# Two transformer layers on one core: the second branch turns moved behind pair 3's query turns, and the last expert's result handled in quarter pieces

## The reference

```python
for l in range(DEPTH):
    h = rms_norm(x, mix_norm_g[l])
    z = h @ w_in[l]                 # u, v (gMLP), c_q, c_kv, k_r (attention), gates
    y_a = gmlp_branch(u, v, ...) @ gm_w_proj[l]      # "pa": u * (W_s v + b), 8 groups
    y_b = mla_branch(c_q, c_kv, k_r, ...) @ mla_w_proj[l]   # "pb": 16 heads, causal
    gates = sigmoid(z[..., OFF_GATE:])
    x = x + (gates[0] * y_a + gates[1] * y_b) @ w_out[l]
    h2 = rms_norm(x, ffn_norm_g[l])
    if l % 2 == 0:
        x = x + swiglu(h2, dense_w_gu, dense_w_down)
    else:                           # top 2 of 8 by router, softmax weights
        for e in range(8):
            y = y + combine[:, e:e+1] * swiglu(h2, w_gu[e], w_down[e])
        x = x + y
```

## Time and profile before

| | us |
|---|---|
| median of 3 runs | 1450.35 (1450.29 to 1450.68) |
| profiled execution | 1450.41 |
| its span | 1448.7 |
| PE busy | 1438.9 |
| DVE busy | 1160.6 |
| ACT busy | 964.0 |

### The profile page before, as it was taken

One profiled execution on the slowest core, in us unless ns is written; L12 is line 12 of the kernel. 1 busy time (PEld: TensorE's weight loads), 2 busy tenths in 40 slices (PEclk: granted clock), 3 DMA queues, 4 the chain that ended last, 5 costly groups with the idle time before them and its releaser, 6 DMA issues.

```text
span 1448.7 us, 19542 instructions
## 1 busy us (share of the span) xinstructions
PE 1438.9 (99%) x6850; PEld 1187.5 (82%) x6850; DVE 1160.6 (80%) x1144; ACT 964.0 (67%) x1053; POOL 44.5 (3%) x53
## 2 busy tenths in 40 slices
PE   9999999999999999999999999999999999999998
PEld 7888788888888888878888888888888888888886
DVE  6977756665546977656998999999989899899997
ACT  6676754444435676754677777777777777777775
POOL 2000003000000000000200000000000000000300
PEclk9999999999999999999999999999999999999999
DMA  9473348955465463447799999999999999999995
GB/s 341 150 237 117 116 149 302 332 178 177 156 219 177 149 230 116 144 147 272 301 394 380 390 361 395 395 361 395 364 394 395 352 401 373 388 391 359 372 368 218
DMA packets 212316, 414.95 MB, mean 286 GB/s; under 512 B 14188, under 2 KB 55528, under 8 KB 212248
## 3 DMA queue, kind: packets, MB, share of 16 engines
q1 hardware_dynamic: 206232, 393.42, 75.0%
q0 software_dynamic: 4976, 16.97, 3.5%
q10 hardware_dynamic: 1040, 3.68, 0.6%
HBM read 398.20 MB, written 15.81 MB: 286 GB/s over the span
## 4 chain that ended last, share of the span: by engine, by line
PE 98%; ACT 1%; DVE 1%; DMA 0%; issue 0%; SPq 0%; ACTq 0%
PE ps L534 89%; PE ps L1083 1%; PE ps L957 1%; PE ps L935 1%; PE ps L795 1%; PE ps L944 1%; PE ps L915 1%; PE ps L934 0%; PE ps L884 0%; PE ps L1064 0%; DMA xres<-in_x 0%; ACT act_hi L1243 0%; PE ps L928 0%; PE ps L850 0%; PE ps L1075 0%; PE ps L913 0%
## 5 line engine op out<-in xcount | busy, mean ns | idle before, releaser
L504 DVE TENSOR_TENSOR w_lo<-raw,w_hi 128x2048 fp32r<-128x2048 f32 (+1 forms) x242 | 515.8, 2141 | 151.4 <-ACT w_hi L499 147.3
L499 ACT ACTIVATE w_hi<-raw 128x2048 fp32r<-128x2048 f32 (+2 forms) x241 | 433.6, 1801 | 215.2 <-PE ps L534 198.1
L534 PE MATMUL ps<-w_hi,act_hi 128*128 128x512 f32 (+1 forms) x1264 | 332.7, 393 | 1.3 <-ACT act_hi L1243 1.1
L534 PE MATMUL ps<-w_hi,act_lo 128*128 128x512 f32 (+1 forms) x1264 | 328.0, 388 | 0.0
L534 PE MATMUL ps<-w_lo,act_hi 128*128 128x512 f32 (+1 forms) x1264 | 325.0, 387 | 0.0
L534 PEld LDWEIGHTS ps<-w_lo,act_hi 128*128 128x128 f32 x1264 | 235.5, 188 | 48.8 <-DVE w_lo L504 0.5
L534 PEld LDWEIGHTS ps<-w_hi,act_lo 128*128 128x128 f32 x1264 | 235.0, 188 | 48.2
L534 PEld LDWEIGHTS ps<-w_hi,act_hi 128*128 128x128 f32 x1264 | 231.0, 188 | 47.0 <-ACT act_hi L1243 1.6
L499 ACT ACTIVATE w_hi<-raw_more 128x2048 fp32r<-128x2048 f32 x96 | 170.7, 1778 | 65.5 <-PE ps L534 64.0
L504 DVE TENSOR_TENSOR w_lo<-raw_more,w_hi 128x2048 fp32r<-128x2048 f32 x96 | 201.1, 2110 | 14.3 <-ACT w_hi L499 12.9
L504 DVE TENSOR_TENSOR w_lo<-raw_low,w_hi 128x2048 fp32r<-128x2048 f32 (+1 forms) x64 | 128.9, 2022 | 12.4 <-ACT w_hi L499 11.3
(11 more groups left out here) (286 smaller groups left out, 1278.7 us busy)
## 6 DMA issues: line engine op xcount, KB each, us to landing
raw<-in_moe_w_gu SPq DMA_DIRECT2D x192, 512.0 KB, 9.7
raw_more<-in_moe_w_gu SPq DMA_DIRECT2D x96, 512.0 KB, 10.0
raw<-in_w_in SPq DMA_DIRECT2D x72, 512.0 KB, 4.5
raw_low<-in_moe_w_gu SPq DMA_DIRECT2D x64, 512.0 KB, 9.6
raw_more<-in_moe_w_down SPq DMA_DIRECT2D x64, 512.0 KB, 6.2
raw<-in_dense_w_gu SPq DMA_DIRECT2D x44, 512.0 KB, 4.9
raw_low<-in_moe_w_down SPq DMA_DIRECT2D x32, 512.0 KB, 8.1
raw<-in_moe_w_down SPq DMA_DIRECT2D x32, 512.0 KB, 5.8
```

The source lines that it names most:

```text
L499: nc.scalar.activation(w_hi[:, self.split_slot(j), 0:n], self.raw(j)[:, 0:n], ACT.Copy).then_inc(self.hi, 1)
L504: nc.vector.tensor_tensor(w_lo[:, c, 0:n], self.raw(j)[:, 0:n], w_hi[:, c, 0:n].bitcast(F32), ALU.subtract).then_inc(self.lo, 1)
L534: return nc.tensor.matmul(dst, a, b, start=start and n == 0, stop=stop and n == 2)
```

## The change

In the mixer's list, for both layers, `a_turns` 1 leaves the second `gb` chunk and goes into the first `pa` chunk, behind its first three matmuls; `qk_turns` 3 and pair 2's normalisation stand in the `gb` chunk at 5 instead of 6.

```diff
         mul(l, "gb", 1, 4, [("split_lo", l, len(chunks) - 2), *slot(4, exps=False), ("k_scale", l, 1), split("split_lo"),
                             ("softmax", l, 3), evac("gb", 1)], split=False,
-            inside=[(2, ("exps", l, 2)), (5, ("a_turns", l, 1)), (6, turn(3)), (6, ("norm_probs", l, 2)),
+            inside=[(2, ("exps", l, 2)), (5, turn(3)), (5, ("norm_probs", l, 2)),
                     (6, split("split_hi"))])
         mul(l, "pa", 0, 0, [*slot(5, exps=False), split("split_lo"), ("softmax", l, 4)],
-            inside=[(4, turn(4)), (4, split("split_hi"))])
+            inside=[(1, ("a_turns", l, 1)), (4, turn(4)), (4, split("split_hi"))])
```

In the last expert, the last pass of (piece 1, half 0) goes behind the last pass of (piece 0, half 1), and the second half of the result is copied by ACT, scattered by PE, and for the second tile of positions added by DVE and stored by SP, in quarters of 256 columns:

```diff
-        END_ORDER = ((0, 0, (0, 1, 2)), (0, 1, (0, 1)), (1, 0, (0, 1, 2)), (0, 1, (2,)), (1, 1, (0, 1, 2)))
+        END_ORDER = ((0, 0, (0, 1, 2)), (0, 1, (0, 1)), (1, 0, (0, 1)), (0, 1, (2,)), (1, 0, (2,)), (1, 1, (0, 1, 2)))
+        LAST = ((0, 0, 512), (1, 0, 512), (0, 512, 1024), (1, 512, 768), (1, 768, 1024))
...
+            def store_last():
+                for i, (t, c0, c1) in enumerate(LAST):
+                    sp.wait_ge(pass_sems[0]["over"], i + 1)
+                    sp.dma_start(out[0, t * P:(t + 1) * P, c0:c1], xres[:, t, c0:c1]).then_inc(out_stored, 16)
...
-                        if (d, hf) == (1, 0):
+                        if (d, hf, passes[-1]) == (1, 0, 2):
                             mm.then_inc(z["half_done"], 1)
...
-                    pe.wait_ge(z["y_half1"], 1)
                     for t in range(TT):
-                        nc.tensor.matmul(ps[:, 2 + t, :], put[:, t * P:(t + 1) * P], y_sb[:, 512:1024], start=True, stop=True
-                                         ).then_inc(z["scattered"], 1)
+                        for quarter, ready in enumerate((z["y_half1"], z["y_end"])):
+                            if not t:
+                                pe.wait_ge(ready, 1)
+                            c = 256 * quarter
+                            bank = (2, 2, 3, 4)[2 * t + quarter]
+                            nc.tensor.matmul(ps[:, bank, c:c + 256], put[:, t * P:(t + 1) * P],
+                                             y_sb[:, 512 + c:768 + c], start=True, stop=True).then_inc(z["scattered"], 1)
...
-                        copy(y_sb[:, 512:1024], ps[:, 7, :], slot_w[:, 0:1]).then_inc(z["y_half1"], 1)
+                        copy(y_sb[:, 512:768], ps[:, 7, 0:256], slot_w[:, 0:1]).then_inc(z["y_half1"], 1)
+                        copy(y_sb[:, 768:1024], ps[:, 7, 256:512], slot_w[:, 0:1]).then_inc(z["y_end"], 1)
...
+                def last_scattered():
+                    for i, (t, c0, c1) in enumerate(LAST):
+                        dve.wait_ge(z["scattered"], (1, 2, 4, 5, 6)[i])
+                        if not c0:
+                            dve.wait_ge(rows_added[1][t], 16)
+                        bank, b0 = ((0, 0), (1, 0), (2, 0), (3, 0), (4, 256))[i]
+                        tt(xres[:, t, c0:c1], xres[:, t, c0:c1], ps[:, bank, b0:b0 + c1 - c0], ALU.add).then_inc(z["over"], 1)
```

More of the change, by code:

```diff
@@ L452, in decoder_trunk @@
                 "eturn_free1", "y_copied", "y_stored", "xs_landed", "first_turned", "first_hi", "first_lo", "slot_read",
-                "put_ready", "put_turned", "put_copied", "half_done", "y_half0", "y_lo", "y_half1", "scattered", "over")})
+                "put_ready", "put_turned", "put_copied", "half_done", "y_half0", "y_lo", "y_half1", "y_end", "scattered", "over")})
         class Ring:
@@ L687, in expert_loads @@
                     r.load(sp, e, GU_CHUNKS + d, [(to[:, 0:half], a), (to[:, half:2 * half], b)])
+            def store_last():
+                for i, (t, c0, c1) in enumerate(LAST):
+                    sp.wait_ge(pass_sems[0]["over"], i + 1)
+                    sp.dma_start(out[0, t * P:(t + 1) * P, c0:c1], xres[:, t, c0:c1]).then_inc(out_stored, 16)
             def store_out(z):
                 for i, (t, hf) in enumerate(TAIL):
-                    sp.wait_ge(z["over"], i + 1 if z is pass_sems[0] else len(TAIL) * (E - 1) + i + 1)
+                    sp.wait_ge(z["over"], len(TAIL) * (E - 1) + i + 1)
                     sp.dma_start(out[0, t * P:(t + 1) * P, hf * 512:(hf + 1) * 512],
@@ L700, in _ @@
             expert_loads(moe_ring, 0, E - 1, True)
-            store_out(pass_sems[0])
+            store_last()
             with sp.If(crowded > P):
-                sp.wait_ge(out_stored, 16 * len(TAIL))
+                sp.wait_ge(out_stored, 16 * len(LAST))
                 sp.dma_start(xs[:], x_rows[0, 1]).then_inc(pass_sems[1]["xs_landed"], 16)
@@ L710, in _ @@
                 store_out(pass_sems[1])
-                sp.wait_ge(out_stored, 2 * 16 * len(TAIL))
-            sp.wait_ge(out_stored, 16 * len(TAIL))
+                sp.wait_ge(out_stored, 16 * (len(LAST) + len(TAIL)))
+            sp.wait_ge(out_stored, 16 * len(LAST))
         @block.gpsimd
@@ L1230, in _ @@
             with pe.If(crowded > P):
-                pe.wait_ge(pass_sems[0]["over"], len(TAIL))
+                pe.wait_ge(pass_sems[0]["over"], len(LAST))
                 moe_pass(moe_ring2, 1)
@@ L2013, in scattered @@
                         dve.wait_ge(z["scattered"], len(TAIL) * (n - 1) + i + 1)
-                        if not q and not hf:
-                            dve.wait_ge(rows_added[1][t], 16)
                         xh = xres[:, t, hf * 512:(hf + 1) * 512]
@@ L2053, in body @@
                             ALU.subtract).then_inc(z["y_lo"], 1)
-                        scattered(1)
+                        last_scattered()
                     elif q:
@@ L2074, in _ @@
             with dve.If(crowded > P):
-                dve.wait_ge(out_stored, 16 * len(TAIL))
+                dve.wait_ge(out_stored, 16 * len(LAST))
                 link(ts(place, place, -float(P), None, ALU.add))
```

## The result

| | before | after |
|---|---|---|
| median, 6 runs each, same chip | 1450.64 (1450.29 to 1452.91) | 1457.05 (1456.74 to 1458.96) |
| profiled execution / its span | 1450.41 / 1448.7 | 1457.01 / 1455.2 |
| ratio | | 1.0045 [1.0035, 1.0055] |

The change costs 6.4 us. The forecast was +4.8 (1455.1, range 1453.0 to 1456.6): the direction is right, the size is outside the range. Of the 1.95 between 1455.1 and 1457.05, 0.3 is that the kernel before has a median of 1450.64 here and had 1450.35 over the three runs that the forecast started from.

A forecast was written before the change was run, and what follows sets the result against it. The prediction took TensorE (PE) to bound the kernel, busy 99% of the span. It added +4.98 us for both layers' waits and -0.2 for the tail to 1450.35, giving 1455.1, range 1453.0 to 1456.6.

The forecast's parts named there:

- What bounds: Whole kernel: PE bounds it, busy 99% of the span and 98% of the chain of work that ended last.
- A: Start of the first matmul of the first `pa` chunk, 584.56 in layer 1 before; forecast to come 1.57 us earlier.
- `t_lo` at A + 5.97: On DVE, the moved `t_lo` starts 5.97 us after A, behind nine instructions that run without a hole.
- +2.49 for a layer: First `pa` chunk: PE waits for `t_lo` at pair 4's query turns, which makes each layer 2.49 us longer.
- the 0.70 saved: Before A, waits around the old place of the branch turns go away, saving 0.70 us a layer.
- The clock: PE's granted clock stays at 1.00 around the turns; a fall to 1.2 GHz got chance 0.04, 5 us a layer.
- The tail, -0.2: Last matmuls, adds and stores: the last add and last store come some 0.2 us sooner, taken as -0.2.
- The upper bound of +0.9: Tail: nothing saved, and the extra issue and smaller packets cost as much as 0.9 us.
- The sum: Whole kernel: +4.98 for both layers and -0.2 for the tail give +4.8 us, 1455.1.
- (a): Pair 4's turns: banks are free before PE asks, only savings count, -1.6 us, 1448.8; chance 0.06.
- (b): Pair 4's turns: the wait is shorter or one layer's is partly absorbed, +2.5 us, 1452.9; chance 0.08.
- (c): Behind the new wait PE's clock falls to 1.2 GHz, 5 us a layer, 1465; chance 0.04.

The follow-up runs named there:

- Part 4: turns_only with pair 4's query turns nine matmuls sooner (turn_sooner, 1463.97 us) or nine later (turn_later, 1453.12 us).
- part 5: turns_only with the weight split and pair 3's exponentials and normalisation moved behind the branch turns; 1448.85 us, ratio 0.9989.
- turns_only: The kernel before with only the moved turns, the tail as before; 1456.39 us, ratio 1.0045.
- turns_again: turns_only, unchanged, run a second time; 1457.7 us, ratio 1.0043 against before.
- lo_first: The kernel of part 5: turns_only with the weight split and pair 3's exponentials and normalisation behind the branch turns; 1448.85 us, ratio 0.9989.
- turn_sooner: turns_only with pair 4's query turns nine matmuls sooner, right behind the branch turns; 1463.97 us, ratio 1.0086 against before.
- turn_later: turns_only with pair 4's query turns nine matmuls later; 1453.12 us, ratio 1.0011 against before.
- fill_eight: turns_only with 8 unused identity turns on PE ahead of pair 4's turns; 1455.78 us, ratio 1.0039 against before.
- fill_wait: turns_only with 20 unused identity turns on PE ahead of pair 4's turns; 1455.15 us, ratio 1.0035 against before.
- tail_only: The kernel before with only the tail's new matmul order and quarter pieces, the turns as before; 1450.76 us, ratio 1.0004.
- order_only: The kernel before with only the new order of the last matmuls; copies, adds and stores as before; 1450.46 us, ratio 1.0.

## Why the prediction was wrong

**What bounds, and A: right.** A was to come 1.57 earlier; corrected for the shift ahead of it, it came 1.51 + 0.13 = 1.64 earlier in layer 0, and 584.56 + 3.97 - 586.88 = 1.65 in layer 1.

**`t_lo` at A + 5.97: right**, 5.95 and 5.94. It was read from nine DVE instructions without a hole, and holds in both layers. Part 4 shows that `t_lo` stays there wherever PE asks for it, part 5 that it comes sooner, and the wait is gone, when the steps ahead of it on DVE and ahead of `t_hi` on ACT are moved.

**+2.49 for a layer: right at full clock**, 2.40 in layer 1 and 2.38 to 2.41 in the layers of `turns_only` and of the two filled waits. It is the wait of 2.83, plus 0.28 between the halves, less the 0.70 saved: 2.41.

**The clock: this step failed.** I wrote that the granted clock is 1.00 and that PE has no wait of 3 us here, and gave the fall 0.04, all or nothing, at 5 us a layer. But a row of 1.00 in a stretch with no wait says nothing of what follows a wait of 2.8. It fell in one layer of the profiled execution of after, in both of `turns_again`, in none of `turns_only`, so in three of six passages seen. The mean clock is 0.998 or less in five of the six executions of after, and in none of the 69 of before that were run beside the experiments. Nor was the price right: I took the 24 matmuls of a whole chunk, but only the eight turns and 12 matmuls stand behind the wait, and the clock comes back among the 12. So it took 1.45 to 1.47 (3.4 us at the low level) or 2.68 (6.9 us), not 5.

For the profiled execution the clock is 1.47 of what lies over the forecast. For the median it is only likely: the waits and the tail give 1450.64 + 4.81 + 0.23 = 1455.7, and two layers with an even chance of some 1.5 each are about the 1.4 that is left. But the one execution of after with a mean clock of 1.000 took 1456.74, so about 1 us can come without the clock, as the late load and the late start of `turns_only` did.

**The tail, -0.2: wrong in sign, small.** The last add did end earlier: the last of DVE's adds lies +5.97 from before where the splits in front lie +6.28, -0.31 where -0.2 was forecast. The failed step is "I take -0.2, what DVE's own end gives": the end of the span is that of the last transfer, and lies +0.23 instead. The upper bound of +0.9 covered it. Copies of 256 columns took 0.47, not the half of 0.69 (0.35) that I worked with, and the scatter started 0.11 sooner (1447.89 - 1441.72 = 6.17 against the splits' 6.28), not 0.2.

**The sum** by what the trace of after measured: 0.13 + 2.41 + 1.47 + 2.40 - 0.13 + 0.23 = 6.5, the growth of the span. Of the 1.7 by which that is more than the forecast 4.8, 1.47 is the clock, 0.43 the tail, 0.13 the start, -0.17 the waits (4.81 for 4.98) and -0.13 lies between.

**Rivals.** (a) falls by the waits; `lo_first` shows what it would have needed: with `t_lo` at A + 2.62 nothing waits and the kernel is 0.11% faster. (b) falls too: neither layer absorbed anything. (c) is right as a mechanism and mis-sized. What stays open is why a wait of the same length lowers the clock in one layer and not in the other.

## What to carry to other kernels

Before moving a step on the bound engine, count what stands ahead of its partner on the engine that frees its buffer: here nine DVE instructions, 6 us, decided, and moving two steps of the list turned +0.45% into -0.11%. A wait of some 3 us on TensorE can cost half as much again through its clock (1.47 for 2.83), or nearly as much again (2.68 for 2.86), and it differed from one execution of the same kernel to the next. So give the fall a probability for each wait, and a price from the matmuls that stand behind the wait. For the end of a kernel, forecast the last transfer, not the last add.

## What the runs showed of the hardware

- With waits of 2.83 to 2.86 us TensorE's granted clock fell to 0.5 in three of six layer passages (`after`, `turns_only`, `turns_again`); with 4.9 us in both that were seen (`turn_sooner`); with 0.8 us in neither (`turn_later`); and not in the four where 8 or 20 small turns stood in the wait (`fill_eight`, `fill_wait`).
- At the low level eight 128-column turns took 1.91 instead of 1.15 in the chain, eight 512-column matmuls 3.16 instead of 2.00 in the timeline of `turns_again` (a part of them at full speed again).
- A fifth store issued by SP took 1.15 to 1.36 us (`after`, `tail_only`) instead of 0.33, and once a third of four took 1.49 (`order_only`).
- A copy of 128x256 from PSUM took ACT 0.47 us, one of 128x512 0.69 (`after`, `before`).
